# Two MLP layers of a fused fp32 encoder: the norm's factor leaves the up-projection's evacuation and is applied to the row sums instead

## What is computed

```
def rmsnorm(x, g, eps=EPS):
    y = xf * lax.rsqrt(jnp.mean(xf * xf, axis=-1, keepdims=True) + eps)
    return (y * g).astype(x.dtype)

def sq_relu_mlp(y, w_up, w_down):
    u = y @ w_up                                   # (528, 1024) @ (1024, 4096)
    return jnp.square(jax.nn.relu(u)) @ w_down     # @ (4096, 1024)

    h = h + sq_relu_mlp(rmsnorm(h, norm_gains[i, 1]), mlp_w_up[i], mlp_w_down[i])
```

## Time and profile before

| | |
|---|---|
| median of 3 runs | 1189.25 us (1189.15 to 1189.55) |
| the profiled execution, its own time | 1188.87 us |
| its span, first to last instruction | 1187.1 us |
| TensorE's mean granted clock | 0.998 |
| busy: TensorE / VectorE / ScalarE / GpSimd | 1176.7 / 957.6 / 740.0 / 118.2 us |
| MLP of layer 0, MLP of layer 1 with its tail | 251 to 597, 840 to 1179 us |

### The profile page before, as it was taken

How to read it: one execution, slowest core, us unless ns; L and a number is a source line. 1 busy time by engine, 2 the same in 40 slices (tenths; PEclk the granted TensorE clock), 3 DMA queues, 4 the chain that set the end, 5 groups by cost and what they waited for, 6 DMA issues and landing times.

```text
span 1187.1 us, 22848 instructions
## 1 busy us (share of the span) xinstructions
PE 1176.7 (99%) x8809; PEld 1126.4 (95%) x8809; DVE 957.6 (81%) x1423; ACT 740.0 (62%) x1305; POOL 118.2 (10%) x177
## 2 busy tenths in 40 slices
PE   9999999999999999999999999999999999999998
PEld 8999999999999999999999999987798999989988
DVE  6889888787888788886568889887878888978853
ACT  6777877745556565555357887787555556656643
POOL 3211120100110110112010000000001001001000
PEclk9999999999999999999999999999999999999999
DMA  7343342432563553565232122214334636446522
GB/s 180 95 107 92 89 101 86 135 122 72 142 144 100 116 144 107 114 184 169 54 90 71 54 71 71 88 36 125 126 107 107 143 108 156 128 125 142 174 96 72
DMA packets 152470, 131.87 MB, mean 111 GB/s; under 512 B 23304, under 2 KB 143168, under 8 KB 152384
## 3 DMA queue, kind: packets, MB, share of 16 engines
q1 hardware_dynamic: 141600, 104.93, 30.7%
q0 software_dynamic: 10656, 25.66, 9.6%
q10 hardware_dynamic: 128, 0.09, 0.0%
HBM read 111.43 MB, written 19.24 MB: 110 GB/s over the span
## 4 chain that ended last, share of the span: by engine, by line
PE 79%; issue 17%; DVE 2%; ACT 1%; POOL 1%; DMA 0%; DVEq 0%; POOLq 0%; ACTq 0%
PE ps L2330 32%; PE ps L2282 21%; PE ps L2047 18%; PE ps L2549 2%; PE ps L2102 1%; PE ps L2120 1%; PE ps L2234 0%; PE ps L2199 0%; DMA meta_in<-in_meta_tokens_dram 0%; PE ps L2188 0%; ACT wh L765 0%; DVE lo L1660 0%; DVE ps L1685 0%; POOL khm L751 0%; PE ps L2063 0%
## 5 line engine op out<-in xcount | busy, mean ns | idle before, releaser
L2047 PE MATMUL ps<-yh,wh 128*128 128x264 f32 (+1 forms) x704 | 160.5, 302 | 0.0
L2047 PE MATMUL ps<-yh,wl 128*128 128x264 f32 (+1 forms) x704 | 155.3, 295 | 0.0
L2047 PE MATMUL ps<-yl,wh 128*128 128x264 f32 (+1 forms) x704 | 155.3, 294 | 0.0
L765 ACT ACTIVATE hi<-lof 128x1024 fp32r<-128x1024 f32 x80 | 82.8, 1054 | 76.8 <-DVE lof L1653 76.8
L2330 PE MATMUL ps<-th,hi 128*128 128x264 f32 (+1 forms) x448 | 127.0, 283 | 0.9 <-ACT pu L765 0.8
L1660 DVE TENSOR_TENSOR lo<-lof,hi 128x1024 fp32r<-128x1024 f32 x80 | 97.0, 1223 | 37.5 <-ACT hi L765 37.5
L2330 PE MATMUL ps<-th,lo 128*128 128x264 f32 (+1 forms) x448 | 126.5, 282 | 0.0
L2330 PE MATMUL ps<-tl,hi 128*128 128x264 f32 (+1 forms) x448 | 126.5, 282 | 0.0
L765 ACT ACTIVATE hi<-raw 128x1024 fp32r<-128x1024 f32 (+1 forms) x128 | 115.3, 915 | 12.3 <-DMA raw<-in_mlp_w_up_dram 8.2
L2282 PE MATMUL ps<-ah,hi 128*128 128x264 f32 (+1 forms) x448 | 115.6, 316 | 0.0
L2282 PE MATMUL ps<-al,hi 128*128 128x264 f32 (+1 forms) x448 | 115.6, 316 | 0.0
(11 more groups left out here) (325 smaller groups left out, 3292.2 us busy)
## 6 DMA issues: line engine op xcount, KB each, us to landing
raw<-in_mlp_w_up_dram SPq DMA_DIRECT2D x32, 1024.0 KB, 6.6
raw<-in_mlp_w_down_dram SPq DMA_DIRECT2D x32, 1024.0 KB, 5.0
raw<-in_diff_w_in_dram SPq DMA_DIRECT2D x24, 512.0 KB, 3.8
raw<-in_mlstm_w_in_dram SPq DMA_DIRECT2D x16, 512.0 KB, 4.6
h_sum<-abuf POOLq DMA_DIRECT2D x24, 264.0 KB, 6.9
h_sum<-abuf POOLq DMA_DIRECT2D x24, 256.0 KB, 7.2
h_sum<-h POOLq DMA_DIRECT2D x16, 264.0 KB, 2.5
h<-h_sum POOLq DMA_DIRECT2D x8, 528.0 KB, 6.0
```

What stands on the lines that cost most here:

```text
L765: return nc.scalar.activation(o, i, ACT.Copy, scale=scale)
L2047: last = mm(ps[:, bank + s, 0:w_], w[:, slot, kb, :], m[:, kb, t0:t0 + w_], start=(kb == 0 and n == 0), stop=(kb == CB - 1 and n == 2))
```

## The change

1. ACT writes the mean square plus eps (an Identity activation) to `ab[1]` before it takes the logarithm. The exponential of an MLP's norm has scale −1, so `rb` holds 1/(ms + eps) = r². `refine_factor` on DVE improves it by one Newton step, at pair 2.
2. `scale_residual` on DVE multiplies h in place by ms + eps, in four instructions of two blocks each, after the weight sums of pair 2 (the third pair). POOL saves h in four DMAs, one behind each, and no longer while the norm is prepared.
3. Up results leave PSUM by a Relu on ACT (`positive`), without a factor. DVE's evacuation of up pairs is gone. `squares` begins with its own `positive`.
4. The squares of pairs 0 and 1 move on ACT to pair 2, in among the snaps of its products; DVE's four `act_lo` for them stand behind C1 of pair 2.
5. The last down results: DVE adds PSUM and h into `tbuf` (`row_sum`), then multiplies by `rb` into h. TensorE waits for `row_sum` where it waited for `m_evac`.

```diff
+                if n % 2:
+                    nc.scalar.activation(tokens(ab[1], spans), src, ACT.Identity, bias=eps_d[:, 0:1], scale=1.0 / D).then_inc(ms_rd, 1)
                 nc.scalar.activation(tokens(rb[:, :], spans), src, ACT.Ln, ...).then_inc(ln_done, 1)
...
-                for k in range(CB):
-                    pool.wait_ge(h_ready, 16 * layer + k + 1)
-                    pool.dma_start(h_sum[k], h[:, k, :]).then_inc(h_saved, 16)
+                for q in range(4):
+                    pool.wait_ge(h_scaled, FACTOR * layer + q + 1)
+                    pool.dma_start(h_sum[2 * q:2 * q + 2, :, t0:T].rearrange("k p t -> p k t"),
+                                   h[:, 2 * q:2 * q + 2, t0:T]).then_inc(h_saved, 16)
...
+                def positive(i, m):
+                    ...
+                    nc.scalar.activation(pair_tokens(tb[m], layer, i), pair_out(layer, i, m), ACT.Relu).then_inc(m_evac, 1)
...
                     if begins:
                         snap(i, "P1")
-                        if is_up(i):
-                            squares(i - 1, 1)
-                        else:
+                        if i == PLAIN:
+                            squares(0, 0)
+                            squares(0, 1)
+                        if not is_up(i):
                             block_hi(i, "S3")
                         snap(i, "P5")
+                        if i == PLAIN:
+                            squares(1, 0)
...
                         snap(i, "U2")
+                    if i == PLAIN:
+                        squares(1, 1)
...
+                def scale_residual():
+                    dve.wait_ge(ms_rd, layer + 1)
+                    for q in range(4):
+                        rows = h[:, 2 * q:2 * q + 2, t_in:T]
+                        V.tensor_tensor(rows, rows, ab[1][:, t_in:T].unsqueeze(1).broadcast_to([P, 2, T - t_in]),
+                                        ALU.mult).then_inc(h_scaled, 1)
...
-                    V.tensor_tensor(tokens(h[:, k, :], spans), src, tokens(h[:, k, :], spans), ALU.add).then_inc(m_evac, 1)
+                    V.tensor_tensor(tokens(tbuf, spans), pair_out(layer, i, m), tokens(h[:, k, :], spans), ALU.add).then_inc(row_sum, 1)
+                    dve.wait_ge(row_sum, 8 * layer + k + 1)
+                    V.tensor_tensor(h[:, k, t_in:T], tbuf[:, t_in:T], rb[:, t_in:T], ALU.mult).then_inc(m_evac, 1)
...
-                V.tensor_tensor(h[:, k, cols], ps[:, j % 2, 0:XH], h[:, k, cols], ALU.add).then_inc(m_evac, 1)
+                V.tensor_tensor(tbuf[:, cols], ps[:, j % 2, 0:XH], h[:, k, cols], ALU.add).then_inc(row_sum, 1)
+                dve.wait_ge(row_sum, tail_count(12, part, j))
+                V.tensor_tensor(h[:, k, cols], tbuf[:, cols], rb[:, cols], ALU.mult).then_inc(m_evac, 1)
...
-                pe.wait_ge(m_evac, tail_count(2 * N_TAKEN - TAIL, part, j - 2))
+                pe.wait_ge(row_sum, tail_count(12, part, j - 2))
```

More of the change, by code:

```diff
@@ L531, in freed @@
                 return m_out, N_OUT * layer + SENT_OUT[i, m]
+            if i >= PAIRS - 4:
+                return row_sum, 8 * layer + 2 * (i - PAIRS + 4) + m + 1
             return m_evac, N_TAKEN * layer + TAKEN[i, m]
@@ L1044, in snap @@
                         copy(pu[:, 1, 0:w], product_bank(layer, i, "S2")).then_inc(p_copied, 1)
+                def positive(i, m):
+                    if not crossed(i):
+                        act.wait_ge(m_done, items + DONE[i, m])
+                    else:
+                        if m == 1:
+                            act.wait_ge(m_done, items + DONE[i, "A22"])
+                        act.wait_ge(c_done, adds + ADDED[i, "C22" if m else "C1"])
+                    wait(act, ah_done, 8 * (4 * layer + i // 8) + 2 * (i % 8) + m - 1)
+                    nc.scalar.activation(pair_tokens(tb[m], layer, i), pair_out(layer, i, m), ACT.Relu).then_inc(m_evac, 1)
                 def squares(i, m):
@@ L1714, in block_lo @@
                                     ALU.subtract).then_inc(b_lo, 1)
-                def evacuate(i, m):
[L1718 to L1727, removed]
-                        wait(dve, ah_done, block_of(i, m) - 1)
-                        V.scalar_tensor_tensor(pair_tokens(tb[m], layer, i), src, 0.0, pair_tokens(rb, layer, i),
-                                               ALU.max, ALU.mult).then_inc(m_evac, 1)
-                        return
+                def scale_residual():
[4 more added lines that the diff above has]
+                                        ALU.mult).then_inc(h_scaled, 1)
@@ new lines, in refine_factor @@
+                def refine_factor():
+                    made, ms, r = FACTOR * layer + 5, ab[1][:, t_in:T], rb[:, t_in:T]
+                    dve.wait_ge(rb_ready, norm + 1)
+                    V.scalar_tensor_tensor(ms, ms, -1.0, r, ALU.mult, ALU.mult).then_inc(h_scaled, 1)
+                    dve.wait_ge(h_scaled, made)
+                    V.scalar_tensor_tensor(r, ms, 2.0, r, ALU.add, ALU.mult).then_inc(h_scaled, 1)
+                    dve.wait_ge(h_scaled, made + 1)
+                def evacuate(i, m):
@@ L1763, in mlp @@
                     up_before = crossed(i - 1) and is_up(i - 1)
-                    if up_before or i > 0 and not is_up(i - 1) and not in_tail(layer, i - 1) and not sent_down(i - 1):
+                    if i > 0 and not is_up(i - 1) and not in_tail(layer, i - 1) and not sent_down(i - 1):
                         evacuate(i - 1, 1)
@@ L1791, in mlp @@
                         total(i, "C1")
-                        if is_up(i):
-                            evacuate(i, 0)
-                    if is_up(i - 1) and not sent_down(i):
+                    if i == PLAIN:
+                        for n in range(4):
+                            act_lo(n // 2, n % 2)
+                    elif i > 1 and is_up(i - 1) and not sent_down(i):
                         act_lo(i - 1, 1)
@@ L1805, in mlp @@
                         split(U_IN1, 0)
-                    if is_up(i) and not crossed(i):
-                        if i > 0:
-                            evacuate(i, 0)
-                        act_lo(i, 0)
-                        evacuate(i, 1)
+                    if i == PLAIN:
+                        refine_factor()
                     elif not is_up(i) and not in_tail(layer, i) and not sent_down(i):
```

33 lines of the change are left out of this document (22 added, 11 removed).

## The result

The changed kernel takes **1197.68 us** (1197.18 to 1197.96, 4 runs) against 1189.40 (1189.15 to 1190.08, 4 runs) in the same comparison: ratio 1.0068, 95% interval 1.0051 to 1.0086. It is slower by 8.3 us. The prediction said slower by 5.85 and 1195.1, range 1191.8 to 1199.5. The direction was right and the size was 2.4 us short. Of the places, pair 3's S2 in both layers, its S1 in layer 0 and the tail's third product were named. The waits before S4 and S3 of pair 2, with the longest of all among them, were not, and the wait before S1 that was named for layer 1 is absent.

A forecast was written before the change was run, and what follows sets the result against it. The kernel was taken as bound by its number of matmuls, TensorE 99% busy. Terms 2.5 + 2.4 − 0.8 + 0 + 1.3 + 0.45 = 5.85 us slower gave 1195.1 us, range 1191.8 to 1199.5.

The forecast's parts named there:

- the wait before S1 that was named for layer 1: Pair 3, layer 1: TensorE was to wait before S1 as well as S2; no separate size given.
- Term 1: Pairs 0 to 3, each layer: ScalarE starts pair 3's high parts late, +2.5 us in layer 0, +2.4 in layer 1.
- bytes move from 271.8 to 277.2 and the save is in at 277.8: Layer 0: eight times 264 KB at 0.68 us each take 5.4 us; the save of h lands at 277.8.
- the prediction's own sign of being wrong: Anywhere in the kernel: the prediction is wrong if, among other signs, TensorE stops at a place not named; no size.
- main case: Whole kernel: slower by 5.85 us, 1195.1 us, own range 1192.5 to 1197, chance 0.68.
- rival (a): Saves of h: queued saves land slowly, 2.4 us more in each layer, 10.7 us slower in all, 1200; chance 0.15.
- nothing else moves then, since the weights of pair 4 are asked for behind pair 2's low parts: Saves of h: no other transfer runs beside them, an argument against slow saves; no size.
- The other landing rule that was cited: Saves of h: 2.0 us + bytes / 436 GB/s, 3.2 us for 528 KB, last save in at 277.4.
- Term 2: The groups' last up pair: DVE loses evacuations, so layer 1's three waits of 0.25 go, −0.8 us.
- DVE was what made P1 late: The groups' last up pair: VectorE's evacuations delay P1, so removing them should clear three waits, −0.8 us.
- Term 3: End of layer 0: a second DVE instruction moves `yl` from 599.84 to 601.3, still in time; cost 0.
- Term 4: Tail of layer 1: longer DVE rounds make the third product wait 1.3 us; the last square comes +0.45 us.

The follow-up runs named there:

- Experiment 1: Changed kernel, with the load of pair 4's weights held back until h is saved: 1197.11 us, ratio 1.0067.
- experiment 8: Changed kernel, with the four saves of each layer issued by SyncE on its own queue instead of by GpSimd: 1195.03 us, ratio 1.0049.
- Experiment 6: The kernel before the change, with ScalarE's copy P1 of the next pair moved ahead of the squares of pair (i, 0): 1185.13 us, ratio 0.9961.
- experiment 10: Changed kernel, with P1 of the next pair first, pair 2's late squares behind pair 3's high parts, and saves on SyncE's queue: 1188.38 us, ratio 0.9994.
- experiment 5: Changed kernel, with next pair's P1 ahead of Relu and squares, and squares of (1, 0), (1, 1) behind pair 3's high parts: 1190.13 us, ratio 1.0004.
- experiment 7: Changed kernel, with only ScalarE's order in pair 2 altered: squares of (1, 0) and (1, 1) behind pair 3's high parts: 1197.14 us, ratio 1.0063.
- experiment 9: Changed kernel, with eight saves of one block instead of four of two: 1197.82 us, ratio 1.007.
- experiment 3: Changed kernel, with the multiplication by r² left out of the last down sums, so one DVE instruction remains: 1196.13 us, ratio 1.006.
- experiment 4: Changed kernel, with ScalarE's copy P1 of the next pair ahead of pair (i, 0)'s Relu and squares: 1193.38 us, ratio 1.0041.

## Why the prediction was right, and by how much it missed

- **Term 1** carried the right mechanism and was mis-sized: 2.5 became 3.5 in layer 0, and 2.4 became 4.06 in layer 1. The step that was mis-sized is "bytes move from 271.8 to 277.2 and the save is in at 277.8": in the prediction's clock (0.38 us added) it was in at 279.0. The duration came from a save that moved alone; four twice that size, queued behind each other, came 4.4 us after their issue in the median and up to 5.5, at 360 GB/s and not 397. In the prediction's clock the first squares start 1.3 us (layer 0) and about 2 us (layer 1) later than counted, and the high parts 1.1 and 1.8 us. Of ScalarE's own work the count held: from the first square to the high parts 284.84 − 278.71 = 6.13 us, forecast 6.3.
- The waits before S4 and S3 of pair 2 follow from the same step. By the prediction's count ScalarE copied P5 at 280.0 and U2 at 282.0, in time for these two products of the kernel before, so that TensorE would not stop:

```profile
280.96 0.28 PE L2330 MATMUL ps<-yh,hi 128*128 128x264 f32 x1
...
282.42 0.28 PE L2330 MATMUL ps<-th,hi 128*128 128x264 f32 x1
```

  With the first square over a microsecond late both copies came too late. These waits meet the prediction's own sign of being wrong, "if TensorE stops at a place not named here". They add little to the time, since S2 of pair 3 hangs on the high parts all the same: it comes 6.75 and 6.67 us behind them, 6.87 and 6.80 before.
- The measured 1197.68 lies above the main case's own range, which ended at 1197, and inside the whole range only by rival (a). The saves came between the two: in layer 0 1.3 us later than the main case has them, where (a) adds 2.4.
- The sentence "nothing else moves then, since the weights of pair 4 are asked for behind pair 2's low parts" was wrong in fact: SyncE issued that load at 276.45, before the saves had landed. Experiment 1 shows that it matters little. The mechanism of rival (a), then, was partly there. GpSimd's queue is one part, for experiment 8 gets 388 GB/s and 1.4 us sooner squares in layer 0. The Trainium skill, "GPSIMD Engine Reference", "Specifications", has GpSimd share SBUF interfaces with VectorE while that reads two SBUF inputs. The experiment agrees with it in direction, but moves the issue as well as the queue, and does not show that this is the cause.
- The other landing rule that was cited, 2.0 us + bytes / 436 GB/s (the Trainium skill, "DMA: Bandwidth & Descriptors", "Anatomy of one DMA"), gives 3.2 us for 528 KB. The first save of each layer landed after 3.2 us, the median of the eight is 4.4: the rule holds for the first in a row of four and not for those queued behind it.
- **Term 2**: −0.8 forecast, −0.85 measured. But "DVE was what made P1 late" tells only half. C1, the evacuation, two squares and P1 stand in one chain. The changed kernel leaves P1 behind the squares and frees VectorE, and the three waits go: in layer 1's first group S2 now starts 3.71 us behind C1's start, where it was 3.01. Experiment 6 leaves VectorE's work as it is and moves P1 ahead of the squares, and they go too. Either was enough.
- **Term 3**: 0 forecast, 0 measured. `yl`, forecast at 601.3 and moved by the 3.11 us of the ledger to 604.4, starts at 604.42.
- **Term 4**: 1.3 forecast, 1.61 measured. The rounds are 1162.54 − 1157.67 = 4.87 us (4.9 forecast), and the slip of 2.6 against TensorE came out as such. The third product's start was read too late, 1160.2 instead of 1160.04: the chain's row at 1154.50 is not the tail's start, whose first matmul stands at 1154.25. The rest is the step from the sum's end to the matmul, which was counted as nothing. The last square's +0.45 is 0.47.

VectorE and ScalarE in the tail's last full rounds, and the last square of the kernel:

```profile
1157.67 0.68 DVE L1770 TENSOR_TENSOR tbuf<-ps,h 128x512 f32<-128x512 f32 x1
...
1162.54 0.68 DVE L1770 TENSOR_TENSOR tbuf<-ps,h 128x512 f32<-128x512 f32 x1
...
1187.89 0.42 ACT L1359 ACTIVATE abuf<-h 128x256 f32<-128x256 f32 x1 [2.02 <-DVE h L2044]
```

What stays open: why the last bytes of layer 1's saves, on either queue, trickle for up to 2 us, why the bytes move more slowly while GpSimd issues, and what holds layer 1's last two waits in experiment 10.

## What to carry to other kernels

Read a wait's releaser one step further back: the copy `pu` was 0.38 us long and never the problem, the two squares queued ahead of it on the same engine were. Moving the short instruction that another engine waits for ahead of the long ones was worth 4.6 us here, while taking 18 us of work from VectorE and giving 36 to ScalarE cost 8.3. When work moves onto an engine in front of a chain, ask for its place in that engine's order before its amount: the same instructions took 7.5 us less in another order (experiment 5). Try such an order on the kernel before as well, or its gain is booked to the change. And price a transfer by the queue in which it will stand, never by one that moved alone.

## What the hardware showed that was not expected

- TensorE's clock after a wait. In the changed kernel, too, the 1.93 us wait in layer 1 was followed by the 1.2 GHz level between 875.2 and 878.6, with matmuls 0.21 apart:

```profile
876.00:877.00 1.00, 1.00 (x5) 1.00 (x6) 0.00 (x0) 0.97 (x3) 0.00 (x0) 0.50 0.00 0
```

  There it most likely cost nothing: the slow matmuls took 1.3 us, but S2 of pair 3 hung on ScalarE's P1 anyway and TensorE still waited 1.16 us for it. In experiment 7 it cost 1.5 us twice. Experiments 1 and 9 had the drop too, behind 2.25 and 2.22 us in the same place. The shorter waits looked at left the clock at 1.00: 1.39 us in experiment 8, 1.61 in the changed kernel's tail. A long wait does not always lower it: experiments 3 and 4 had one of 2.45 and one of 1.92 in the same place and kept 1.00.
- A queue of four saves ends unevenly: some 2 us at 0.03 to 0.11 of the DMA engines' time behind the last full window (experiment 1).
